# Solving four tiles at a time in the chunk inverse of an RWKV-7 recurrence

## What is computed

```python
def step(S, inp):
    r_t, w_t, k_t, v_t, kk_t, a_t = inp
    S = (S * w_t[:, :, None, :]
         - jnp.einsum('bhvk,bhk->bhv', S, kk_t)[..., None] * (kk_t * a_t)[:, :, None, :]
         + v_t[..., None] * k_t[:, :, None, :])
    return S, jnp.einsum('bhvk,bhk->bhv', S, r_t)
```

## Time and profile before

| | |
|---|---|
| median of 3 runs | 2360.72 us (2359.28 to 2361.04) |
| time of the profiled execution | 2361.71 us |
| span in its trace | 2359.9 us |
| TensorE busy | 90% of the span |
| mean granted TensorE clock | 0.919 of full speed |
| matmul records of lines 1014, 1021, 1026 | 1600, 1600, 1280 |

### The profile page before, as it was taken

One profiled execution on the slowest core, in us unless ns is written; L12 is line 12 of the kernel. 1 busy time (PEld: TensorE's weight loads), 2 busy tenths in 40 slices (PEclk: granted clock), 3 DMA queues, 4 the chain that ended last, 5 costly groups with the idle time before them and its releaser, 6 DMA issues.

```text
span 2359.9 us, 44326 instructions
## 1 busy us (share of the span) xinstructions
PE 2115.1 (90%) x19733; PEld 1803.2 (76%) x19733; DVE 865.4 (37%) x1741; ACT 691.7 (29%) x1407; POOL 487.5 (21%) x238
## 2 busy tenths in 40 slices
PE   5999788788889999999989987977879899999996
PEld 3987467348559999999978854853765799999995
DVE  1521544744334331333152226455451533123312
ACT  3323443543122111211142245444420312112112
POOL 1233000200003333333222310011000233333330
PEclk8999789679999999999989987976899999999998
DMA  9463200000021223322366430000001122332111
GB/s 304 155 157 116 54 2 3 3 1 4 20 71 54 77 64 88 85 62 73 114 202 183 128 89 1 4 3 2 3 4 54 54 79 60 85 85 77 50 49 45
DMA packets 238034, 163.09 MB, mean 69 GB/s; under 512 B 21634, under 2 KB 235380, under 8 KB 237332
## 3 DMA queue, kind: packets, MB, share of 16 engines
q1 hardware_dynamic: 236404, 158.29, 23.3%
q0 software_dynamic: 1440, 1.97, 0.3%
HBM read 157.09 MB, written 3.15 MB: 68 GB/s over the span
## 4 chain that ended last, share of the span: by engine, by line
PE 77%; DVE 9%; ACT 5%; issue 3%; DMA 2%; SPq 0%; POOL 0%; DVEq 0%; ACTq 0%
PE PS L767 24%; PE PS L768 24%; PE PS L713 7%; PE PS L930 3%; PE PS L1021 2%; PE PS L1014 2%; PE PS L714 2%; PE PS L1026 2%; PE PS L903 2%; DMA ring<-in_w_in 2%; PE PS L733 1%; PE PS L913 1%; DVE mix L1619 1%; DVE negm L1622 1%; DVE mix L1651 1%
## 5 line engine op out<-in xcount | busy, mean ns | idle before, releaser
L620 POOL TENSOR_TENSOR wsplit<-ring,wsplit 128x1024 fp32r<-128x1024 f32 (+1 forms) x120 | 325.8, 2715 | 784.8 <-ACT wsplit L1215 784.8
L767 PE MATMUL PS<-h_hi,wsplit 128*128 128x320 f32 x1408 | 426.9, 311 | 21.6 <-ACT h_hi L1191 17.7
L768 PE MATMUL PS<-h_hi,wsplit 128*128 128x320 f32 x1408 | 426.0, 310 | 0.0
L1215 ACT ACTIVATE wsplit<-ring 128x1024 fp32r<-128x1024 f32 (+1 forms) x120 | 137.3, 1146 | 725.4 <-PE PS L768 725.4
L767 PEld LDWEIGHTS PS<-h_hi,wsplit 128*128 128x128 f32 x1408 | 266.4, 189 | 23.4 <-issue 18.1
L768 PEld LDWEIGHTS PS<-h_hi,wsplit 128*128 128x128 f32 x1408 | 266.4, 189 | 0.0
L767 PE MATMUL PS<-h_lo,wsplit 128*128 128x320 f32 x704 | 217.1, 309 | 0.0
L768 PE MATMUL PS<-h_lo,wsplit 128*128 128x320 f32 x704 | 217.1, 309 | 0.0
L768 PE MATMUL PS<-hid_hi,wsplit 128*128 128x320 f32 x704 | 212.1, 309 | 0.0
L767 PE MATMUL PS<-hid_hi,wsplit 128*128 128x320 f32 x704 | 212.0, 309 | 0.0
L767 PE MATMUL PS<-in_hi,win 128*128 128x320 f32 x544 | 172.7, 325 | 26.0 <-ACT in_hi L1191 17.9
(11 more groups left out here) (285 smaller groups left out, 3924.3 us busy)
## 6 DMA issues: line engine op xcount, KB each, us to landing
ring<-in_w_ada SPq DMA_DIRECT2D x48, 1024.0 KB, 7.2
ring<-in_ffn_w_in SPq DMA_DIRECT2D x88, 512.0 KB, 5.0
ring<-in_ffn_w_out SPq DMA_DIRECT2D x32, 704.0 KB, 4.7
ring<-in_w_in SPq DMA_DIRECT2D x8, 1024.0 KB, 8.0
ring<-in_w_in SPq DMA_DIRECT2D x10, 512.0 KB, 7.6
ring<-in_w_in SPq DMA_DIRECT2D x16, 256.0 KB, 5.7
ring<-in_w_out SPq DMA_DIRECT2D x16, 256.0 KB, 8.2
ring<-in_w_out SPq DMA_DIRECT2D x8, 512.0 KB, 9.7
```

Source lines behind the costliest of these rows:

```text
L620: nc.gpsimd.tensor_tensor(lo, raw_w, hi, SUB).then_inc(wl_ready(), 1)
L767: mm(lat[:, 0:TH], w, v[:, 0:TH], start=(n == 0), stop=(n == total - 1))
L768: last = mm(cx[:, 0:TH], w, v[:, TH:T], start=(n == 0), stop=(n == total - 1))
L1215: act(hi, raw_w, ACT.Copy).then_inc(wh_ready(), 1)
```

## The change

The identity is put into the stored factor. VectorE adds it to B-A and to X of the start in one operation over four 64x64 blocks (line 1669 of the changed kernel), and the masks `lvl` of levels 1 to 5 get a diagonal of ones. A masked product is then identity plus update, so that the new inverse is a plain product, and nothing is summed in PSUM over levels. The identity's matmuls at the start go: one transpose per matrix is left, four matmuls for a pair where there were eight.

Head 1 changes sides: its Y lives on the other partition half, and the two products that cross over write from one half to the other (`other` in the code, where `own` stays on its half). Head 1's X comes out of the bank `ps[2p+1]` and is copied by VectorE (line 1681, 64 columns), while ScalarE copies three blocks, 192 columns, from `ps[2p]`. Line numbers of the changed kernel are 7 to 19 higher around here; line 1008 issues all of its level matmuls.

```diff
         TOK = [mix[:, b:b + 512].rearrange("p (a t) -> p a t", a=4) for b in pb]
-        XY = [mix[:, b + 512:b + 768].rearrange("p (a t) -> p a t", a=4) for b in pb]
-        LP = [mix[:, b + 768:b + 1280].rearrange("p (h a t) -> p h a t", h=2, a=4) for b in pb]
-        P1 = [mix[:, b + 1280:b + 1408].rearrange("p (a t) -> p a t", a=2) for b in pb]
-        T0 = [mix[:, b + 1408:b + 1536].rearrange("p (a t) -> p a t", a=2) for b in pb]
+        XY = [mix[:, b + 768:b + 1024].rearrange("p (a t) -> p a t", a=4) for b in pb]
+        LPH = [[mix[:, b + 512 + 512 * hd:b + 768 + 512 * hd].rearrange("p (a t) -> p a t", a=4) for hd in range(2)]
+               for b in pb]
+        LPV = [mix[:, b + 512:b + 1536].rearrange("p (h q) -> p h q", h=2)[:, :, 0:256].rearrange(
+            "p h (a t) -> p h a t", a=2) for b in pb]
+        XBA = [mix[:, b + 640:b + 1280].rearrange("p (h q) -> p h q", h=2)[:, :, 0:256].rearrange(
+            "p h (a t) -> p h a t", a=4)[:, :, 0:4:3, :] for b in pb]
+        TM = [mix[:, b + 1280:b + 1408].rearrange("p (a t) -> p a t", a=2) for b in pb]
...
+        Y0, X0, Y1, X1 = range(4)
+        W0, W1, Y1_LAST = X0, Y1, X1
...
-                        halves = [(hd, ck, rows_of[ck]) for hd in range(2) for ck in range(2)]
+                        own, other = (((0, 0), (1, 1)), ((0, 1), (1, 0)))
+
+                        def tiles(out, lhsT, rhs, way):
+
+                            for a, b in way:
+                                last = mm(out[rows_of[b], :], lhsT[rows_of[a], :], rhs[rows_of[a], :],
+                                          start=True, stop=True)
+                            return last
+
                         for n, (p, d, t) in enumerate(group):
-                            e.wait_ge(lp_sb.sem, lp_sb.upto(l, base + n + 1))
-                            e.wait_ge(t0_sb.sem, t0_sb.upto(l, base + n + 1))
-                            b1 = ps[2 * p + 1]
-                            for hd, ck, cs in halves:
-                                mm(b1[cs, 64 * hd:64 * hd + 64], T0[p][cs, hd, :], eye64[cs, :],
-                                   start=(hd == 0), stop=False, skip_group_check=True)
-                            for hd, ck, cs in halves:
-                                last = mm(b1[cs, 128 + 64 * hd:192 + 64 * hd], eye64[cs, :], T0[p][cs, hd, :],
-                                          start=False, stop=False, skip_group_check=True)
-                            last.then_inc(xy_ps(), 1)
+                            e.wait_ge(eye_sb.sem, eye_sb.upto(l, base + n + 1))
+                            tiles(ps[2 * p][:, 0:64], XY[p][:, X0, :], eye64, own)
+                            tiles(ps[2 * p + 1][:, 0:64], XY[p][:, X1, :], eye64, other).then_inc(xy_ps(), 1)
                         gx = 6 * base
                         for lv in range(1, 6):
                             at = 5 * base + (lv - 1) * ng
                             for n, (p, d, t) in enumerate(group):
                                 e.wait_ge(xy_sb.sem, xy_sb.upto(l, gx + (lv - 1) * ng + n + 1))
-                                for hd, ck, cs in halves:
-                                    last = mm(ps[2 * p][cs, 64 * hd:64 * hd + 64], LP[p][cs, hd, BA, :],
-                                              XY[p][cs, 2 + hd, :], start=True, stop=True)
-                                last.then_inc(p1_ps(), 1)
+                                if lv > 1:
+                                    e.wait_ge(x1_sb.sem, x1_sb.upto(l, at - ng + n + 1))
+                                tiles(ps[2 * p][:, 192:256], LPH[p][0][:, BA, :], XY[p][:, X0, :], own)
+                                tiles(ps[2 * p + 1][:, 192:256], LPH[p][1][:, BA, :], XY[p][:, X1, :],
+                                      other).then_inc(p1_ps(), 1)
                             for n, (p, d, t) in enumerate(group):
                                 e.wait_ge(p1_sb.sem, p1_sb.upto(l, at + n + 1))
-                                b1 = ps[2 * p + 1]
-                                for hd, ck, cs in halves:
-                                    mm(b1[cs, 64 * hd:64 * hd + 64], P1[p][cs, hd, :], XY[p][cs, hd, :],
-                                       start=False, stop=(lv == 5), skip_group_check=True)
-                                for hd, ck, cs in halves:
-                                    at_x = slice(128 + 64 * hd, 192 + 64 * hd)
-                                    if lv < 5:
-                                        last = mm(b1[cs, at_x], XY[p][cs, hd, :], P1[p][cs, hd, :],
-                                                  start=False, stop=(lv == 4), skip_group_check=True)
-                                    else:
-                                        last = mm(b1[cs, at_x], LP[p][cs, hd, KA, :],
-                                                  TOK[p][cs, tV, 64 * hd:64 * hd + 64], start=True, stop=True)
+                                b0, b1 = ps[2 * p], ps[2 * p + 1]
+                                tiles(b0[:, 0:64], TM[p][:, 0, :], XY[p][:, Y0, :], own)
+                                if lv < 5:
+                                    tiles(b1[:, 0:64], XY[p][:, Y1, :], TM[p][:, 1, :], other)
+                                    tiles(b0[:, 128:192], TM[p][:, 1, :], XY[p][:, Y1, :], own)
+                                    last = tiles(b0[:, 64:128], XY[p][:, Y0, :], TM[p][:, 0, :], own)
+                                else:
+                                    tiles(b1[:, 0:64], TM[p][:, 1, :], XY[p][:, Y1, :], other)
+                                    tiles(b0[:, 64:128], LPH[p][0][:, KA, :], TOK[p][:, tV, 0:64], own)
+                                    last = tiles(b0[:, 128:192], LPH[p][1][:, KA, :], TOK[p][:, tV, 64:128], own)
                                 last.then_inc(xy_ps(), 1)
                         for n, (p, d, t) in enumerate(group):
 
                             e.wait_ge(xy_sb.sem, xy_sb.upto(l, gx + 5 * ng + n + 1))
-                            for hd, ck, cs in halves:
-                                last = mm(ps[2 * p][cs, 128 * hd:128 * hd + 128], XY[p][cs, hd, :],
-                                          a_and_w1(p, cs, hd), start=True, stop=True)
+                            e.wait_ge(x1_sb.sem, x1_sb.upto(l, 5 * base + 4 * ng + n + 1))
+                            for hd in range(2):
+                                for r in rows_of:
+                                    last = mm(ps[2 * p][r, 128 * hd:128 * hd + 128], XY[p][r, (Y0, Y1_LAST)[hd], :],
+                                              a_and_w1(p, r, hd), start=True, stop=True)
                             last.then_inc(ug_ps(), 1)
...
                         for lv in range(6):
                             for n, (p, d, t) in enumerate(group):
                                 e.wait_ge(xy_ps.sem, xy_ps.upto(l, 6 * base + lv * ng + n + 1))
-                                act(XY[p].rearrange("p a t -> p (a t)"), ps[2 * p + 1][:, 0:256],
-                                    ACT.Copy).then_inc(xy_sb(), 1)
+                                if lv == 0:
+                                    act(XY[p][:, Y0:X1:2, :], PS[:, 2 * p:2 * p + 2, 0:64], ACT.Copy).then_inc(xy_sb(), 1)
+                                else:
+                                    act(XY[p][:, Y0:X1, :], ps[2 * p][:, 0:192].rearrange("p (a t) -> p a t", a=3),
...
-                            V.tensor_tensor(P1[p], PS[:, 2 * p:2 * p + 2, 256:320],
+                            V.tensor_tensor(XY[p][:, X0:X1 + 1:2, :], PS[:, 2 * p:2 * p + 2, 256:320],
                                             lvl[:, d, 0:1, :].to_broadcast([128, 2, 64]), MUL).then_inc(l0_sb(), 1)
-                            V.tensor_tensor(LP[p].rearrange("p h (a b) t -> p h a (b t)", a=2),
+                            V.tensor_tensor(LPV[p],
                                             PS[:, 2 * p:2 * p + 2, 0:256].rearrange("p h (a t) -> p h a t", a=2),
                                             masks[:, d, :].unsqueeze(1).unsqueeze(1).to_broadcast([128, 2, 2, 128]),
                                             MUL).then_inc(lp_sb(), 1)
                             e.wait_ge(l0_sb.sem, l0_sb.upto(l, base + n + 1))
-                            V.tensor_tensor(T0[p], P1[p], eye64[:, :].unsqueeze(1).to_broadcast([128, 2, 64]),
-                                            ADD).then_inc(t0_sb(), 1)
+                            e.wait_ge(lp_sb.sem, lp_sb.upto(l, base + n + 1))
+                            V.tensor_tensor(XBA[p], XBA[p],
+                                            eye64[:, :].unsqueeze(1).unsqueeze(1).to_broadcast([128, 2, 2, 64]),
+                                            ADD).then_inc(eye_sb(), 1)
                         for lv in range(1, 6):
                             at = 5 * base + (lv - 1) * ng
                             for n, (p, d, t) in enumerate(group):
                                 e.wait_ge(p1_ps.sem, p1_ps.upto(l, at + n + 1))
```

(7 more changed lines are left out.)

14 lines of the change are left out of this document (8 added, 6 removed).

## The result

The changed kernel takes 2375.4 us (2371.7 to 2381.1 in five runs) against 2359.3 us before: 1.0077 [1.0055, 1.0099], so 0.8% slower, where 1.1% faster was forecast. Its profiled execution took 2375.4 us too.

A forecast was written before the change was run, and what follows sets the result against it. TensorE was taken to set the level alone in groups of four, a loop of latencies in groups of two. Eight groups at 2.45 (19.6 us) plus four at 1.4 (5.7) save 25.3: 2335 us, range 2325 to 2348.

The forecast's parts named there:

- start: First transpose to first masking of a level: group of four saves 0.55 us, loses 1.00 in VectorE's factors.
- levels: First masking to line 1045's first matmul: 2.90 us saved a group of four; in twos, 1.28 plus 0.1.
- tail: Line 1045's first matmul to the group's last of line 1080, in the chain over the chunks: no change.
- The price of a tile slot (0.117 us): Level products: one matmul per used tile costs 0.117 us with two tiles or four; 4 slots a pair, not 6.
- The level, 2.18: Group of four: a level repeats after 2.18 us against 2.79, last first products waiting for ScalarE's copy.
- The forecast's loop: Group of two: latencies through TensorE, VectorE and ScalarE make a level 1.69 us, against 2.01.
- All of it reaches the end: Behind each recurrence: the whole 25.3 us saving shows, since TensorE's, ScalarE's and VectorE's next work is queued there.
- The factors, 0.25 a pair: VectorE's factor stage: 0.13 us for more elements plus 0.12 for a wait, 1.00 lost in a group of four.
- The clock stays 1.00: Levels: TensorE keeps full clock, as the new levels have denser matmul records than the old group of two.
- its rival's: Levels: gaps drop the clock to 1.2 GHz, a level takes 3.7 us, kernel near 2390; chance 0.05.
- The tiles do run together: Level products: rival had `own` and `other` taking turns, 2364 us; chance 0.13 together with the four-slot case.
- ScalarE's pace: Rival: ScalarE's copies, 0.44 us apart, set a level of 2.45 us in groups of four, 2344; chance 0.10.

The follow-up runs named there:

- a_two: Changed kernel with two tiles as before (head 1 kept on its own partition half), identity still in the factor: 2391.1 us, 1.0118.
- a_pool_two: Changed kernel with the identity's addition on GpSimd and two tiles as before: 2365.4 us, 1.0008.
- a_pool: Changed kernel with the addition of the identity moved from VectorE to GpSimd: 2357.1 us, 0.9981.
- b_prep: Kernel before, its factor stage slowed by a wait for the operation ahead and one more VectorE addition: 2387.2 us, 1.0107.
- a_warm: Changed kernel with two wide unused matmuls between the identity transposes of successive pairs in the factors: 2369.5 us, 1.0036.
- L67: Stream of 512 small matmuls without waits, nothing else computed, four tiles as in the changed kernel: 26.5 us from first start to last.
- L72: Same kind of matmul stream with four tiles, a bank for each row half: 27.0 us from first start to last.

## Why the prediction was wrong, point by point

The forecast was 25.3 us less in the traces' terms: start 3.4 more, levels 28.7 less, tail even. Measured: start 7.7 more, levels 2.7 less, tail 8.0 more. The misses are 4.3, 26.0 and 8.0. Two assumptions of the term for the levels failed: that a slot's price is a pace, and that the clock stays.

**The price of a tile slot (0.117 us): right in a burst, wrong as a pace. This is the first step that failed.** The row it came from the earlier trace rows is a short stage, in steps of four matmuls, which can live on what is in store. A level is 96 records for four pairs. At the supply's 3.45 to 3.73 us for 128 that is 2.6 to 2.8 us, and the old level of 2.79 was already there; four of the 32 passages from level to level in groups of four already took 3.0 to 3.6 us before. "TensorE alone sets it" was not the whole of it: array and supply had nearly the same pace, and doubling the one left the other. The bounds of the forecast had no such case, and no rival was the supply.

**The level, 2.18:** right where clock and instructions are there (2.16 and 2.17). So were the copies (0.33 and 0.22), the three slots of the second products (copies of ScalarE start 0.35 apart, 1.38 for four of 0.33), and the end of TensorE's wait at line 1397. In a group of two 1.76 was measured at full clock (forecast 1.69), and 2.25 at half clock, which is more than the 2.01 before. The forecast's loop put 0.05 us between VectorE's end and the second products, where the earlier trace rows has 0.10 (398.56 to 398.66).

**"All of it reaches the end": wrong.** In the tail lines 1045 to 1062 wait 7.4 us for issue, against 1.6 before: what the levels use up of the supply is missing there. a_two against the changed kernel shows 5.7 us of it, a_pool_two against a_pool 4.5. The other 2.3 us of the tail's 8.0 are there with two tiles too.

**The factors, 0.25 a pair: too small.** The pace is 1.33 and not 1.25. Line 1669 takes 0.43 (forecast 0.41), and starts 0.11 behind the end of line 1663's operation (335.00 to 335.11; forecast 0.04). With 40 pairs that is 3 us, most of the 4.3. The term was small, but what hangs on it was put at nothing: with the addition off VectorE in both kernels, the change costs 2.1 us and not 16.1.

**"The clock stays 1.00": the second step that failed, and for another reason than its rival's.** The density of the levels was weighed, and these are indeed denser. But the clock falls at the factors, whose transposes the change halved while VectorE's work grew, and half clock reaches 2.0 to 6.6 us into the levels of every group, where it reached into none before. b_prep, with eight transposes and factors as slow, has 16 us of it in the levels, the changed kernel 46. The rival's price came near: it had 3.7 us for a level of four at half clock, and 3.47 was measured, 0.7 more than before and not 0.9. a_warm wins 10 us of the 26 back.

**The tiles do run together**, also with both row halves in one bank (2.09 us for 128 records with one bank as with two) and in the mixed sequence (3.01). The Trainium skill, TensorEngine Tiling (Array Packing), section Gotcha 1: PSUM Pressure, says that different row tiles cannot access the same PSUM bank simultaneously. That is not borne out where they write different halves of its partitions (2.09 us in both streams). **ScalarE's pace** was no limit.

**How the 26 us split.** From the first masking of one level to that of the next there are 48 passages. In the changed kernel 28 of them are wholly at full clock; they lie 10.5 us in all above the undisturbed 2.16 and 1.76 us, and hold 7.5 us of waits for issue. The other 20 have half clock in them; they lie 15.3 us above, and hold no wait for issue. So 10.5 us of the miss stand with the supply and 15.3 with the clock. But the two are tied, since at half clock the supply catches up: a_warm, with nearly all of the half clock gone, wins 10.0 us, and its waits for issue grow. What each alone would cost is not measured.

Not settled: what sets the 3.45 to 3.73 us of a packet (in the stream of L67 a packet starts 1.0 to 1.4 us behind TensorE's resuming, takes 0.9 to 1.3 us, and TensorE resumes 1.3 to 1.5 us behind its end), how many are held in store (159 records ran ahead of the first gap in L67, 255 in L72), and whether the recorder, which was on in every run here, has a part in it.

## What to carry to other kernels

Ahead of making small matmuls faster, count their instructions: here a stretch that used 256 of them in less than about 3.5 us ran dry once its store was spent, and the stage that waited was in part a later one. Read the price of a burst and the pace of a stream from different rows. And look at what TensorE does in the stage before the one that is made faster: work taken out of a thin stage can cost the next one its clock, and one operation more on the engine that TensorE waits for there can cost as much as faster matmuls win (here an addition that an idle GpSimd does as well).

## What the runs showed of the hardware that was not expected

- TensorE's instructions come in packets of 16 KB, 256 instructions, no faster than one in 3.45 to 3.73 us in four-tile streams of 64 columns; such streams of float32 matmuls stand still for 1.4 us in the mean behind every 128 records (9.9 us in seven gaps).
- At half clock a 64x64 float32 matmul with 32 columns costs as much as one with 64 (0.64 us for the second products of a pair), and the clock stayed at 0.50 through the levels with such products (170 us, masks of zero in that run), where with 64 columns it came back to 1.00 within them.
- An operation of VectorE that waits for the one right ahead starts 0.11 us behind its end, where 0.04 was seen elsewhere.
- GpSimd adds 128x256 float32 elements in 0.64 us beside VectorE's masking, and the masking is not slowed (0.68, as before).
